# Attention scores from rounded parts, and the first row maxima moved into the projection stage

## The reference

```python
s = einsum(q, k) * HEAD_DIM ** -0.5          # kind 0: main keys only where |q - k| <= 128
p = softmax(concat([s_main, s_ctx, sink]))   # the sink stands in kind 0 alone
o = einsum(p, v)
```

## Time and profile before

| | us |
|---|---|
| time, median of 3 runs | 3229.28 |
| lowest, highest | 3226.82, 3235.23 |
| span of the profiled execution | 3215.5 |
| first layer: last turn to first score (276.5 to 295.2) | 18.7 |
| first layer: first score to last product (295.2 to 445.3) | 150.1 |
| second layer: last projection to first score (1265.4 to 1283.6) | 18.2 |
| second layer: first score to last product (1283.6 to 1391.6) | 108.0 |

### The profile page before, as it was taken

How to read it: one execution, slowest core, us unless ns; L and a number is a source line. 1 busy time by engine, 2 the same in 40 slices (tenths; PEclk the granted TensorE clock), 3 DMA queues, 4 the chain that set the end, 5 groups by cost and what they waited for, 6 DMA issues and landing times.

```text
span 3215.5 us, 50344 instructions
## 1 busy us (share of the span) xinstructions
PE 2983.4 (93%) x21802; PEld 1880.8 (58%) x21802; DVE 1100.8 (34%) x1930; ACT 737.7 (23%) x1393; POOL 381.7 (12%) x494
## 2 busy tenths in 40 slices
PE   6999989699999998986988888999999999999999
PEld 3645556455555464554433333888865568678887
DVE  4124754211111244643222224322434463232242
ACT  3113651000000133541000002222322362222232
POOL 2022520122222121411000000000000000000000
PEclk8998989799999999997999999999999989999999
DMA  8930033899999810037999996122311202231130
GB/s 342 394 129 1 1 144 120 344 401 409 408 409 408 308 55 1 1 138 290 417 423 423 424 423 252 59 105 79 113 67 55 69 18 79 79 111 65 66 140 30
DMA packets 138400, 626.97 MB, mean 195 GB/s; under 512 B 12592, under 2 KB 19776, under 8 KB 82896
## 3 DMA queue, kind: packets, MB, share of 16 engines
q1 hardware_dynamic: 122064, 577.67, 44.8%
q0 software_dynamic: 16128, 46.18, 4.3%
HBM read 607.36 MB, written 16.45 MB: 194 GB/s over the span
## 4 chain that ended last, share of the span: by engine, by line
PE 42%; DMA 10%; DVE 2%; ACT 1%; issue 1%; SPq 0%; POOL 0%; DVEq 0%; ACTq 0%; POOLq 0%
PE bank L959 19%; DMA slots<-in_w_up_dram 10%; PE bank L1526 7%; PE bank L1714 4%; PE bank L1403 3%; PE bank L1630 3%; PE bank L1283 1%; PE bank L1647 1%; PE bank L1424 1%; PE bank L1658 0%; PE bank L1453 0%; PE bank L1648 0%; SPq L910 0%; PE bank L1060 0%; PE bank L1061 0%
## 5 line engine op out<-in xcount | busy, mean ns | idle before, releaser
L1403 PE MATMUL bank<-slots,HT 128*32 128x256 f32 x8192 | 478.0, 383 | 52.4 <-DMA slots<-in_w_gate_dram 24.2
L1403 PEld LDWEIGHTS bank<-slots,HT 128*32 128x32 f32 x8192 | 265.6, 111 | 269.0 <-issue 62.6
L959 PE MATMUL bank<-hT_high,chunk_high 128*128 128x512 f32 (+2 forms) x736 | 285.1, 387 | 5.3 <-DVE hT_low L2500 5.3
L959 PE MATMUL bank<-hT_high,low_slots 128*128 128x512 f32 (+2 forms) x736 | 287.1, 390 | 0.0
L959 PE MATMUL bank<-hT_low,chunk_high 128*128 128x512 f32 (+2 forms) x736 | 285.5, 388 | 0.0
L2091 ACT ACTIVATE arena<-bank 128x512 f32<-128x512 f32 x32 | 19.1, 597 | 756.2 <-PE bank L1403 433.8
L959 PE MATMUL bank<-slots,HT 128*128 128x512 f32 (+4 forms) x544 | 180.3, 491 | 7.2 <-issue 5.8
L2843 DVE TENSOR_TENSOR arena<-bank,arena 128x512 f32<-128x512 f32 x32 | 22.1, 692 | 441.9 <-ACT arena L2091 441.9
L959 PEld LDWEIGHTS bank<-hT_high,chunk_high 128*128 128x128 f32 x736 | 139.0, 189 | 35.7 <-DVE hT_low L2500 5.7
L959 PEld LDWEIGHTS bank<-hT_low,chunk_high 128*128 128x128 f32 x736 | 138.8, 189 | 32.4 <-issue 0.2
L959 PEld LDWEIGHTS bank<-hT_high,low_slots 128*128 128x128 f32 x736 | 138.7, 188 | 29.7
(11 more groups left out here) (453 smaller groups left out, 4897.4 us busy)
## 6 DMA issues: line engine op xcount, KB each, us to landing
slots<-in_w_gate_dram SPq DMA_DIRECT2D x128, 1024.0 KB, 19.5
slots<-in_w_up_dram SPq DMA_DIRECT2D x128, 1024.0 KB, 21.7
arena<-in_w_down_dram SPq DMA_DIRECT2D x80, 1024.0 KB, 23.3
arena<-in_ada_w_dram SPq DMA_DIRECT2D x48, 1024.0 KB, 9.1
X<-in_w_down_dram SPq DMA_DIRECT2D x32, 1024.0 KB, 18.3
slots<-in_w_in_dram SPq DMA_DIRECT2D x15, 2048.0 KB, 8.9
slots<-in_ffn_w_gate_dram SPq DMA_DIRECT2D x10, 2048.0 KB, 8.5
slots<-in_ffn_w_up_dram SPq DMA_DIRECT2D x10, 2048.0 KB, 8.9
```

Of the source, the lines that this page charges most:

```text
L959: mm = pe.matmul(out_, lhsT, rhs, start=(n == 0), stop=(n == len(pairs) - 1))
L1403: mm = pe.matmul(bank[32 * j:32 * j + 32, 2 + n, 256 * g:256 * g + 256], xT[:, 64 * k + 32 * g:64 * k + 32 * g + 32], columns(w[:, c, :], ...
```

## The change

1. **Scores.** Each fp32 score product becomes two fp32r products into the same PSUM bank. The first is 128 partitions deep: `k_parts` holds the low part of the keys (key minus rounded key) in partitions 0 to 63 and the rounded keys in 64 to 127, and it meets the rounded queries, which stand in both halves. The second meets the rounded keys (65 deep, with the row of ones) with `q_low`, the low part of the queries, whose partition 64 now takes the shift. ACT makes the rounded copies, once more for partitions 64 to 127 (`round_again`), and DVE makes the two low parts (`low_parts`); `scores` waits for them at a group's first step (`w_split`).
2. **Band and context rows.** The band product uses rounded operands (`ident_high`, `band_high`), and the row scores of context groups use rounded operands (`c_round`).
3. **First group.** In both layers the value products of tiles 3, 4 and 5 come last now. Those of tile 3 stand ahead of the last turn; after it, PE makes two units of the first group's row scores behind each half of tiles 4 and 5, and DVE reduces them, all before `attend` is entered. Rounded operands of this group have tensors of their own (`first_k`, `first_q`). Only two pairs of banks serve these eight units, where four did.
4. **Sink.** For kind 0, ACT copies the shift first and makes the sink's row from the copy afterwards.
5. The scratch for POOL's DMA descriptors is set to 8192 bytes, which makes room for the new tensors.

```diff
-                    unit.pair = (4, 0, 2, 6)[units % 4] if main else (2, 6)[len(group.units)]
+                    unit.pair = (2, 4)[units % 2] if main else (2, 6)[len(group.units)]
...
+        band_high = sb("band_high", [P, 2, P], F32R)
+        ident_high = sb("ident_high", [P, P], F32R)
+        first_k = sb("first_k", [P, NTOK], F32R)
+        first_q = sb("first_q", [P, 2, SEQ], F32R)
...
+        c_round = rounded("c_round", slots_at, first_slots("qkv")[0] % SLOTS * SLOT + 4 * NTOK, 2, 2, CTX)
+        assert 4 * NTOK + 4 * CTX <= SLOT
+        k_parts = rounded("k_parts", arena_at, at_moe, 2, 2, NTOK)
+        q_low = [rounded(f"q_low{l}", slots_at, unit % SLOTS * SLOT, 2, HEADS, NTOK) for l, unit in enumerate(first_slots("w_out"))]
...
-                for i in range(VALUES_LAST[st.layer], ST + CT):
-                    project(i, 2, 384, 512)
+                attention = stage_behind(st)
+                rows = attention.facts["groups"][0].units
+                for j in range(2):
+                    values(VALUES_LAST, j)
                 turned(ST + CT - 1)
+                for b in (2, 4):
+                    pe_may_fill(pe, st, b, 2)
+                done = 0
+                for i in range(VALUES_LAST + 1, ST + CT):
+                    for j in range(2):
+                        values(i, j)
+                        for unit in rows[done:done + 2]:
+                            row_scores(attention, unit)
+                        done += 2
+                assert done == len(rows)
...
+                        pe.wait_ge(sem["w_split"], st.at("w_split", group.split_by))
                         pe.wait_ge(sem["shift_done"], st.at("shift_done", group.number + 1))
-                    keys = K_ext[0:HD + 1, group.kind, group.g, tile_cols(one.kt)]
+                    both_parts = k_parts[:, group.kind, group.g, tile_cols(one.kt)]
+                    high_part = k_high(st, group)[0:HD + 1, tile_cols(one.kt)]
...
                         if j is None:
-                            pe.matmul(bank[:, b, :].rearrange("p (a n) -> p a n", a=2), keys,
-                                      q_ext[0:HD + 1, group.kind, group.heads:group.heads + 2, SEQ:NTOK],
-                                      start=True, stop=True).then_inc(sem["score_full"], 1)
+                            out_ = bank[:, b, :].rearrange("p (a n) -> p a n", a=2)
+                            pe.matmul(out_, both_parts, c_round[:, group.turn, :, :], start=True, stop=False)
+                            pe.matmul(out_, high_part, low[0:HD + 1, group.kind, group.heads:group.heads + 2, SEQ:NTOK],
...
-                        mm = pe.matmul(bank[:, b, 0:one.hi - one.lo], keys, q_ext[0:HD + 1, group.kind, group.heads + j, one.lo:one.hi],
-                                       start=True, stop=not edges)
+                        out_ = bank[:, b, 0:one.hi - one.lo]
+                        pe.matmul(out_, both_parts, q_high(st, group, slice(0, P), j)[:, one.lo:one.hi], start=True, stop=False)
+                        mm = pe.matmul(out_, high_part, low[0:HD + 1, group.kind, group.heads + j, one.lo:one.hi], start=False, stop=not edges)
...
-                            mm = pe.matmul(bank[:, b, lo:lo + P], ident[:, :], band[:, side, :], start=False, stop=t == edges[-1][0])
+                            mm = pe.matmul(bank[:, b, lo:lo + P], ident_high[:, :], band_high[:, side, :], start=False, stop=t == edges[-1][0])
...
+                ahead = st.facts["ahead"]
                 turn_shift(groups[0])
+                if ahead == 2:
+                    for unit in groups[1].units:
+                        row_scores(st, unit)
                 scores(groups[0].steps[0])
...
+                    if i == ST:
+                        first_queries()
+                first_keys()
+                for i in range(VALUES_LAST, ST + CT):
+                    act.wait_ge(sem["full0"], at_bank(st, 0, 2 + i - VALUES_LAST))
+                    take_values(i).then_inc(sem["free0"], 1)
+                    if i == VALUES_LAST:
+                        take_turned(last)
+                        act.wait_ge(sem["free7"], at_bank(st, 7, last))
+                        act.activation(k_parts[HD:P, 1, 0, :], K_ext[0:HD, 1, 0, :], ACT.Copy).then_inc(sem["w_high"], 1)
...
+                    shift = q_low[st.layer][HD:HD + 1, group.kind, group.heads:group.heads + 2, group.queries[0]:group.queries[1]]
                     act.wait_ge(sem["shift_full"], st.at("shift_full", group.number + 1))
+                    act.activation(shift, bank[0:1, 4:6, 0:n], ACT.Copy).then_inc(sem["shift_done"], 1)
...
+                def round_again(group):
+
+                    kind, g = group.kind, group.g
+                    q, q_to = operands(group)
+                    if group.main:
+                        act.wait_ge(sem["rounded"], st.at("rounded", group.split_by - 1))
+                        act.activation(k_parts[HD:P, kind, g, :], K_ext[0:HD, kind, g, :], ACT.Copy).then_inc(sem["w_high"], 1)
+                    act.activation(q_to[HD:P, :, :], q, ACT.Copy).then_inc(sem["w_high"], 1)
...
-                        if n == 1 and to_round and group.main:
-                            round_operands(to_round.pop(0))
+                        if n == 1:
+                            if group.later:
+                                round_again(group.later)
+                            if group.number + ahead + 1 < len(groups):
+                                round_operands(groups[group.number + ahead + 1])
...
+            def low_keys(st, group):
+
+                k = slice(0, HD), group.kind, group.g
+                dve.wait_ge(sem["w_high"], st.at("w_high", group.split_by))
+                dve.tensor_tensor(k_parts[k], K_ext[k], k_high(st, group)[0:HD, :].bitcast(F32), ALU.subtract).then_inc(sem["w_split"], 1)
...
+            def low_parts(st, group):
+
+                if group.main:
+                    low_keys(st, group)
+                low_queries(st, group)
...
+                attention = stage_behind(st)
+                first = attention.facts["groups"][0]
+                low_queries(attention, first)
+                for unit in first.units:
+                    maximum(attention, unit)
...
+                ahead = st.facts["ahead"]
+                low_keys(st, groups[0])
+                if ahead == 2:
+                    for unit in groups[1].units:
+                        maximum(st, unit)
                 for group in groups:
                     units = groups[group.number + ahead].units if group.number + ahead < len(groups) else []
-                    for unit in units:
-                        maximum(unit)
+                    for n, unit in enumerate(units):
+                        maximum(st, unit)
+                        if n == 1:
+                            low_parts(st, groups[group.number + 1])
                         tap_some(1)
+                    if not units and group.number + 1 < len(groups):
+                        low_parts(st, groups[group.number + 1])
...
+    nc = bacc.Bacc("TRN2", target_bir_lowering=False, num_devices=1, dynamic_dma_scratch_size=8192)
```

240 lines of the change are left out of this document (140 added, 100 removed).

## The result

| | median, us | lowest, highest | runs |
|---|---|---|---|
| before | 3229.44 | 3226.82, 3235.23 | 4 |
| after | 3265.55 | 3257.62, 3280.06 | 4 |

After stands to before as 1.0115, with a 95% interval of 1.009 to 1.014: 36 us slower, where 47 us faster were forecast. The traced execution of after took 3258.01 us, near the fastest of its runs.

The account below looks back on a forecast made before the run. PE was taken to bound both attention stages. Savings of 10 + 6 + 30.2 + 22.0 less 8, 6 and 7.5 coming back made 46.7 us less, so 3182 us, with 8 in 10 between 3150 and 3209.

Parts of the forecast that it names:

- The starts: First group's row maxima made among the last values: first score 10 us earlier in the first layer, 6 in the second.
- The new wait at the turn of tile 3: Second layer, ahead of attention: PE has nothing left before this turn and waits 3.6 us.
- The products: Cheaper score, context and band products in attention: 30.2 us saved in the first layer, 22.0 in the second, at full clock.
- rival C: Attention: PE's clock falls more often, four added waits costing 12 to 27 us; put at 3203 us, chance 0.22.
- C's sign: A clock below 0.85 in either attention stage would mean rival C.
- Rival D: PE at half clock throughout both attention stages: 3336 us, slower; decided at a mean clock of 0.72; chance 0.03.
- What comes back: Attention: new DVE and ACT work makes PE wait, costing 8, 6 and 7.5 us.
- The gates for `q_low`: First layer, groups 2, 4 and 6: PE's next main score waits some 2.6 us for DVE's subtractions, 8 us together.
- DVE's pace: Main steps of attention: DVE needs 3.4 us against PE's 3.3, so DVE sets the pace by a little.
- the worst case: First layer: POOL slows DVE's subtractions, so each gate is at worst 2 us longer, 6 in all.
- rival E: Change eaten: POOL's DMAs wait for scratch in expert stages, or gates double and clock falls; 3215 to 3250 us, chance 0.07.
- my own test: If the attention stages are as said and the whole is not, the expert stages have changed and rival E holds.

Follow-up runs that it names:

- e3: The kernel after with row scores 65 deep behind the first group and ACT's second copies right behind the first: 3231.56 us, ratio 0.9981.
- e1: The kernel before with all row scores 64 partitions deep instead of 65: 3265.75 us, ratio 1.0118.
- e6: e3 with the first score product made three times, the first two results overwritten: 3237.21 us, ratio 1.0007.
- e2: The kernel before with only the scratch for POOL's DMA descriptors set to 8192 bytes: 3230.8 us, ratio 0.9987.
- e5: The kernel after with scores back in one fp32 product and row scores 65 deep behind the first group: 3209.15 us, ratio 0.9928.

## Why the prediction was wrong

In the traces attention got 25 us slower where 47 us faster were forecast, a miss of 72. Of these, 31 are the products, 45 the clock, and 5 go the other way as gaps.

**The starts** came out right, the first with some luck. Forecast 285.0 for the first score, measured 284.3; but the last turn began at 267.1 instead of 270.1, and the way from it to the first score took 17.2 us instead of 14.9. In the second layer 6 us were forecast and 4.8 found. The new wait at the turn of tile 3 was 3.43 us where I had 3.6, and PE in time in after shows it below, behind the gates at the first scores of groups 2 and 4:

```profile
323.77 0.79 PE L1261 MATMUL bank<-q_round,k_parts 128*128 128x512 f32 x1 [2.94 <-DVE q_low L2709]
371.69 0.80 PE L1261 MATMUL bank<-q_round,k_parts 128*128 128x512 f32 x1 [2.42 <-DVE q_low L2709]
...
1282.00 1.54 PE L1181 MATMUL bank<-ident,arena 128*128 128x128 f32 x6 [3.43 <-DVE arena L2765]
```

**The products** failed first: "Sums: 30.2 us in the first layer, 22.0 us in the second". The single prices were right (0.23 us a product), but the sum left out that the row scores went from 65 to 64 partitions deep. That edit stands in the full diff of the two kernels (`[0:HD + 1]` became `[0:HD]`) and I took it for nothing. Measured were 13.8 and 7.3 us less work. With the depth undone (e3) it is 25.7 and 19.9, and the depth alone (e1) costs 16.7 and 16.5. The last 4.5 and 2.1 us of the miss no run separates.

**The clock** failed next, as the size of rival C: "Four falls cost 12 to 27 us" counted only long waits that could be named. It cost 45 us more than before in after (24.0 and 21.4), and the forecast itself had it at nothing. The record of the clock has 4 and 1 stretches at the low level in the two stages of before, and 11 and 5 in those of after. At 66 us for 16 of them a fall costs 4.1 us, within the 3 to 7 that I had; their number was wrong, 11 more instead of 4. In e6 added products brought the clock back with the same work on the other engines, so counting new waits can't size it. The stages' clocks, 0.75 and 0.78, are below the 0.85 that I had named as C's sign. Rival D's point, a mean of 0.72, was worked out for 173 us of work in both stages; there were 203, with which the same sum gives 0.85, and the mean was 0.76.

**What comes back** was forecast as 21.5 us and measured as 16.5 more gaps (13.0 and 3.5), near in sum but made up otherwise. The gates for `q_low` stood at two of the three places, 2.94 and 2.42 us where 2.6 was forecast. PE's waits in after's first stage:

```profile
PE bank L1282 <- ACT HT L2049: 12.9, 9, 3.4
PE bank L1261 <- DVE q_low L2709: 5.4, 2, 2.9
```

The first line was 5.0 us before (L1954), so most of the rest lies with ACT's outcome copies, not with DVE's pace. POOL did slow the gate: the queries' low part of group 4 took 2.28 us beside POOL, and the same subtraction 1.21 in the second layer with POOL idle, where I had 1.2:

```profile
369.36 2.28 DVE L2709 TENSOR_TENSOR q_low<-slots,q_round 64x1024 fp32r<-64x1024 f32 x1
...
1349.64 1.21 DVE L2709 TENSOR_TENSOR q_low<-slots,q_round 64x1024 fp32r<-64x1024 f32 x1
```

That is 1.1 us more for a gate, where the worst case had 2; the two gates were 2.94 and 2.42 us with it. In e3, with PE faster, the gaps rise by 32 us, so the term was too small for the case that it was made for.

**The scratch and the expert stages** (rival E) are nothing (e2). The longer expert stage of after's trace would have led me to E by my own test ("if the stages are as said and the whole is not"); it was the execution traced before that was out of line.

Together: -15.7 at the starts, -21.1 work, +45.4 clock, +16.5 gaps make +25 us in the traces; the medians say 36, in part since the traced run of after is 8 us below its median.

## What to carry to other kernels

Compare the depth in partitions of every product in a diff, also where only a row of zeros goes: a pair of products 64 deep between deeper ones cost 0.38 us more, which is more than the pair itself (0.35), and with products 128 deep between its own it cost up to 1.06. When PE gets less to do and the others more, price clock and gaps together: split each stage into work, clock and gaps, and see whether added idle products cost anything; if they don't, the next gain lies in the other engines' order. Here moving one pair of subtractions on DVE gave some 23 us, and with it the change is 29 us faster than before; without the split scores it is 23 us faster (e5), which these runs can't tell apart. And compare clocks over several executions, not in one trace.

## What the runs showed of the hardware

- Row scores 64 deep cost 0.38 us for each unit that stands among products 65 and 128 deep, and 1.06 where band products 128 deep stand between them (e1). Among themselves they keep their usual pace, as in the first group of after, PE in time:

```profile
269.71 0.50 PE L1165 MATMUL bank<-first_k,first_q 64*128 64x512 f32 x1
270.05 0.28 PE L1172 MATMUL bank<-first_k,first_q 64*128 64x256 f32 x1
270.17 0.40 PE L1165 MATMUL bank<-first_k,first_q 64*128 64x512 f32 x1
270.41 0.28 PE L1172 MATMUL bank<-first_k,first_q 64*128 64x256 f32 x1
270.62 2.05 PE L991 MATMUL bank<-slots,HT 128*128 128x128 f32 x16
```

  The first takes 0.34 us, the two in the middle 0.12 and 0.24, the last 0.21: the extra comes at the change of depth, both ways.
- PE took 39 us of additional products in some 8 us (e6), with a granted clock of 0.90 instead of 0.80 and 0.77.
- A subtraction on DVE with two operands in SBUF (64x1024) took 2.28 us beside POOL and 1.21 with POOL idle; the one of 64x768 took 0.94 beside POOL and 0.95 with POOL idle (after, L2698 at 368.49 and 1348.77).
- The first expert stage took 505.8 us in one execution and 523 to 526 in twelve others of twelve kernels, in which PE paused inside each expert without a wait that the profile names. The DMA share was 1.00 and 0.99, and the rate 397 GB/s in the one and 385 in e2's. What set the rate is open.
